# A two-block transformer kernel: three of its linears take both activation parts in one 512-column matmul, and VectorE adds the halves

## The reference

```
x = first_block(x):  proj = rms_norm(x) @ w_in        # 2048 -> 6144; 24 column tiles of 128 here,
                                                      # 24 more as "conv" beside the attention
                     mix  = [attention | gated short conv] @ w_out
                     x += rms_norm(mix);  x += rms_norm((silu(hn @ w_gate) * (hn @ w_up)) @ w_down)
second_block(x):     proj = rms(h) @ w_in_2
                     y_a, y_b = rwkv7(...), fox_attention(...)
                     merged = sigmoid(g_a) * (y_a @ w_branch_a) + sigmoid(g_b) * (y_b @ w_branch_b)
                     h = h + merged @ w_o
                     h = h + (silu(rms(h) @ w_gate) * (rms(h) @ w_up)) @ w_down
```

## Time and profile before

| what | value |
|---|---|
| median of 3 executions | 2859.67 us (2857.73 to 2863.03) |
| profiled execution | 2861.01 us, its span 2859.0 us |
| TensorE busy (matmul) | 2823.2 us, 99% of the span |
| TensorE weight load | 2494.8 us, 87% |
| VectorE busy | 1717.7 us, 60% |
| ScalarE busy | 1226.9 us, 43% |
| DMA | 484.97 MB, mean 170 GB/s |
| granted TensorE clock | 0.998 of full speed over the span |

### The profile page before, as it was taken

The page is one execution under the profiler, slowest core; times in us unless marked ns, Lnnn a source line. Parts: engine busy times, 40 slices in busy tenths (PEclk is TensorE's granted clock), DMA queues, the critical chain, the costliest instruction groups (busy, mean ns, idle before and its releaser), DMA issues.

```text
span 2859.0 us, 49983 instructions
## 1 busy us (share of the span) xinstructions
PE 2823.2 (99%) x20901; PEld 2494.8 (87%) x20901; DVE 1717.7 (60%) x2507; ACT 1226.9 (43%) x1828; POOL 53.1 (2%) x102
## 2 busy tenths in 40 slices
PE   9999999999999999999999999999999999999999
PEld 8999878888888888899788888999998888888887
DVE  6467747666556544654666665766666666565444
ACT  5355544333333444543543443554453333333443
POOL 1000000000000000000000000000000000000000
PEclk9999999999999999999999999999999999999999
DMA  7566455555555555455434335545555555555554
GB/s 246 191 168 180 148 177 162 191 178 189 190 184 183 191 191 190 155 177 163 119 105 125 105 96 162 133 120 192 182 178 188 188 190 177 191 191 163 190 191 147
DMA packets 370319, 484.97 MB, mean 170 GB/s; under 512 B 12360, under 2 KB 181655, under 8 KB 370151
## 3 DMA queue, kind: packets, MB, share of 16 engines
q1 hardware_dynamic: 362752, 471.49, 52.6%
q0 software_dynamic: 4112, 7.88, 1.0%
q10 hardware_dynamic: 3302, 3.39, 0.4%
HBM read 475.70 MB, written 7.01 MB: 169 GB/s over the span
## 4 chain that ended last, share of the span: by engine, by line
PE 89%; DVE 7%; ACT 2%; issue 1%; DMA 1%; DVEq 0%; SPq 0%; ACTq 0%
PE psum L353 20%; PE psum L355 10%; PE psum L565 6%; PE psum L357 5%; PE psum L359 5%; PE psum L358 5%; PE psum L569 5%; PE psum L567 5%; PE psum L694 4%; PE psum L696 4%; PE psum L695 4%; PE psum L763 3%; PE psum L762 3%; PE psum L764 3%; DVE w_lo L343 3%
## 5 line engine op out<-in xcount | busy, mean ns | idle before, releaser
L343 DVE TENSOR_TENSOR w_lo<-w_raw,w_hi 128x1024 fp32r<-128x1024 f32 x728 | 859.6, 1222 | 817.0 <-ACT w_hi L334 817.0
L334 ACT ACTIVATE w_hi<-w_raw 128x1024 fp32r<-128x1024 f32 x728 | 733.0, 1054 | 1160.0 <-PE psum L355 587.1
L353 PE MATMUL psum<-act,w_hi 128*128 128x512 f32 x2816 | 989.8, 394 | 5.1 <-DVE w_lo L343 2.6
L355 PE MATMUL psum<-act,w_lo 128*128 128x256 f32 x2816 | 790.8, 281 | 0.0
L353 PEld LDWEIGHTS psum<-act,w_hi 128*128 128x128 f32 x2816 | 529.6, 188 | 132.4 <-DVE w_lo L343 12.1
L355 PEld LDWEIGHTS psum<-act,w_lo 128*128 128x128 f32 x2816 | 530.1, 188 | 0.1
L357 PE MATMUL psum<-act,w_hi 128*128 128x256 f32 (+3 forms) x1360 | 387.9, 285 | 3.5 <-DVE w_lo L343 3.5
L565 PE MATMUL psum<-act,w_hi 128*128 128x256 f32 (+1 forms) x1280 | 387.5, 303 | 0.3 <-issue 0.3
L359 PE MATMUL psum<-act,w_lo 128*128 128x256 f32 (+3 forms) x1360 | 387.1, 285 | 0.0
L358 PE MATMUL psum<-act,w_hi 128*128 128x256 f32 (+3 forms) x1360 | 387.0, 285 | 0.0
L569 PE MATMUL psum<-act,w_lo 128*128 128x256 f32 (+1 forms) x1280 | 360.9, 282 | 0.0
(11 more groups left out here) (397 smaller groups left out, 2767.7 us busy)
## 6 DMA issues: line engine op xcount, KB each, us to landing
w_raw<-w_in SPq DMA_DIRECT2D x128, 1024.0 KB, 5.8
w_raw<-w_down SPq DMA_DIRECT2D x88, 1024.0 KB, 5.1
w_raw<-w_gate_up SPq DMA_DIRECT2D x88, 1024.0 KB, 5.1
w_raw<-w_gate SPq DMA_DIRECT2D x44, 1024.0 KB, 5.2
w_raw<-w_up SPq DMA_DIRECT2D x44, 1024.0 KB, 5.2
w_raw<-w_out SPq DMA_DIRECT2D x16, 1024.0 KB, 5.3
w_raw<-w_o SPq DMA_DIRECT2D x16, 1024.0 KB, 5.0
w_raw<-w_branch_a SPq DMA_DIRECT2D x8, 1024.0 KB, 5.1
```

Of the source, the lines that this page charges most:

```text
L334: nc.scalar.activation(w_hi[:, s % 2, 2 * h:2 * h + 2, 0:wd], w_raw[:, s % RAW, 2 * h:2 * h + 2, 0:wd], ACT.Copy).then_inc(hi_ready, 1)
L343: nc.vector.tensor_tensor(w_lo[:, s % 2, 2 * h:2 * h + 2, 0:wd], w_raw[:, s % RAW, 2 * h:2 * h + 2, 0:wd], w_hi[:, s % 2, 2 * h:2 * h + 2, ...
L353: pe.matmul(dst.rearrange("p (h n) -> p h n", h=2), w1, both_parts, start=first, stop=False, skip_group_check=True)
L355: return pe.matmul(dst[:, 0:n], w0, act_hi[:, k, tok], start=False, stop=last, skip_group_check=True)
```

## The change

`w_in` (the first 24 tiles of the input linear), `branch` and `w_o` join the list of wide linears. Their tiles take 512 columns of PSUM. The evacuations add the halves:

- `w_in`: four tensor_reduce of 512 to 256 columns and one multiply of the four tiles by rstd, in the place of four multiplies. The mixer waits for the multiply (`proj_done`) and not for `acc_free`.
- `branch`: for each tile a tensor_reduce into SBUF, a wait for it, and a multiply by the gate in SBUF, in the place of one multiply out of PSUM.
- `w_o`: for each tile an add of the lower half to the residual, a wait for it, and an add of the upper half, in the place of one add.

```diff
-        wide = [L[n] for n in ("ffn", "ffn2")]
+        wide = [L[n] for n in ("w_in", "ffn", "branch", "w_o", "ffn2")]
...
-        def take_tiles(lin, i, g, dst, op1=None):
-
-            for m in range(4):
-                wait_tile(lin, i, g, m)
-                nc.vector.tensor_tensor(dst(m), psum[:, first_bank(lin, i, g) + m, 0:SEQ], rstd[:, X],
-                                        ALU.mult).then_inc(acc_free, 1)
-
...
+        proj_done = sem("proj_done")
...
             side(4)
-            pe.wait_ge(acc_free, L["w_in"].t1)
+            pe.wait_ge(proj_done, L["w_in"].iters)
...
-            tiles = [(psum[:, first_bank(lin, 0, 0) + m, 0:SEQ], m * P, P, m) for m in range(4)]
+            tiles = [(psum[:, first_bank(lin, 0, 0) + m], m * P, P, m) for m in range(4)]
...
+        by_gates, half_added, sums_added = sem("by_gates"), sem("half_added"), sem("sums_added")
...
                 b = first_bank(lin, i, g) + m
-                v.tensor_tensor(dst, psum[:, b:b + 1, 0:SEQ], gate_tiles[KT * g + 4 * i + m], ALU.mult) \
-                    .then_inc(acc_free, 1)
+                v.tensor_reduce(dst.rearrange("p k n -> p (k n)"), psum[:, b].rearrange("p (h n) -> p n h", h=2),
+                                AX, ALU.add).then_inc(acc_free, 1)
+                v.wait_ge(acc_free, lin.t0 + 8 * i + 4 * g + m + 1)
+                v.tensor_tensor(dst, dst, gate_tiles[KT * g + 4 * i + m], ALU.mult).then_inc(by_gates, 1)
             if g == 1:
-                v.wait_ge(acc_free, lin.t0 + 8 * i + 8)
+                v.wait_ge(by_gates, 8 * i + 8)
                 part = merged[:, 4 * i:4 * i + 4]
                 v.tensor_tensor(part, part, gated, ALU.add).then_inc(merged_done, 1)
...
                 t, b = res[:, bass.ds(4 * i + m, 1), X], first_bank(lin, i, g) + m
-                v.tensor_tensor(t, psum[:, b:b + 1, 0:SEQ], t, ALU.add).then_inc(acc_free, 1)
+                v.tensor_tensor(t, psum[:, b:b + 1, 0:SEQ], t, ALU.add).then_inc(half_added, 1)
+                v.wait_ge(half_added, 4 * i + m + 1)
+                v.tensor_tensor(t, psum[:, b:b + 1, SEQ:2 * SEQ], t, ALU.add).then_inc(acc_free, 1)
...
-                take_tiles(lin, i, g, lambda m: proj[:, bass.ds(4 * i + m, 1), :])
+                add_halves(lin, i, g, lambda m: proj[:, bass.ds(4 * i + m, 1), :].rearrange("p k n -> p (k n)"))
+                part = proj[:, bass.ds(4 * i, 4), :]
+                v.wait_ge(acc_free, lin.t0 + 4 * i + 4)
+                v.tensor_tensor(part, part, rstd[:, X].unsqueeze(1).broadcast_to([P, 4, SEQ]), ALU.mult) \
+                    .then_inc(proj_done, 1)
```

## The result

The changed kernel takes 2865.15 us (median of 16 executions), the kernel before 2858.72 us (16 executions beside them): a ratio of 1.0023, interval 1.0016 to 1.0030, or 6.4 us more. A second set on another chip gave 1.0019 (1.0010 to 1.0028). So the changed kernel is slower, by about the least that can be told. The profiled execution of the changed kernel has a span of 2864.0 us against 2859.0.

A forecast was written before the change was run, and what follows sets the result against it. TensorE, busy 99%, was taken to bound the kernel by its pace and gaps. Terms -5.1 + 1.6 + 0.8 + 3.2 + 1.7 + 1.9 = +4.1 us gave 2863.8 us against the median of 2859.67, range 2859.0 to 2868.0.

The forecast's parts named there:

- The gain, -5.1: w_in, branch, w_o: 55 units counted, each 0.093 us faster when wide, -5.1 us in all.
- End of w_in, nothing: End of w_in: last reduce and multiply end at 167.5, before TensorE asks at 168.26; no loss, cover 0.7 us.
- Inside branch, +1.6 and +0.8: Branch: w_lo 0.53 us late in three second halves, +1.6; first evacuation starts late, +0.8.
- The gap in front of w_o, +3.2: Passage from branch to w_o: w_lo ends at T + 14.01 (T: the mark, ScalarE's w_hi start), 3.2 us late.
- The clock, +1.7: Behind the 3.2 us gap at w_o: clock falls to 0.50, costing 1.7 us; bounds 0 and 3.4.
- an idle of 1.83 us left the clock at 1.00: At 1388 to 1390 in the earlier profile: evidence that gaps shorter than 1.83 us bring no clock fall.
- The passage to ffn2, +1.9: Passage from w_o to ffn2: longer adds uncovered, two gaps of some 1.3 and 0.8 us, +1.9; no clock fall.
- the clock falls more often or longer: Rival, gaps before w_o and ffn2: more low-clock stretches at 1.7 us each, time 2866.3; chance 0.20.
- The dearer wait for VectorE's own result: Rival, branch pairs: waiting costs 0.16 us, not 0.04; sum +7.0, time 2866.7; chance 0.12.
- Everything added is hidden: Rival, all late places: added VectorE work costs nothing, only the gain of -5.1 stays, 2854.6 us; chance 0.13.

The follow-up runs named there:

- e4: The changed kernel once more, nothing altered, run and profiled a second time; 2864.54 us, ratio 1.0019 to the kernel before.
- e8: The changed kernel with the w_lo of w_o's second unit ahead of branch's last evacuation in VectorE's order; 2865.59 us, ratio 1.0025 to the kernel before.
- e2: The changed kernel with only branch wide, w_in and w_o as before; 2865.51 us, ratio 1.0021 to the kernel before.
- e3: The changed kernel with only w_o wide, w_in and branch as before; 2860.36 us, ratio 1.0001 to the kernel before.
- e6: The changed kernel with the last 4 tiles of branch (fourth iteration, second half) narrow; 2861.25 us, ratio 1.0007 to the kernel before.
- e1: The changed kernel with only w_in wide, branch and w_o as before; 2858.10 us, ratio 1.0001 to the kernel before.

## Why the prediction was right, and where not

The forecast was 2863.8 us, and 2865.15 was measured, inside the range; the sum was +4.1 and the medians say +6.4, the marks +5.2 and, in e4, +4.1. I gave a change of no more than 0.2% the larger chance (0.58), and 0.23% came. The mechanism is the one that was forecast, at each of its places: the pace, the late w_lo behind longer evacuations, and a fall of the clock behind the largest gap and not behind the others. That the sum is so near owes something to luck: w_in brought 0.6 us less than counted and branch lost 0.5 us less, which cancel, and the price of the clock was read wrongly. Step by step:

- **The gain, -5.1.** The pace is as forecast: 5.59 us a wide unit, and 1.3 us over the 14 units of w_o. In w_in it was over-counted. From the fifth unit on, 20 units gave 1.4 us and not 1.9; four of them, which share TensorE with other matmuls, went from 7.31 to 7.27 us, 0.05 each; and a first evacuation that I had not worked out by itself holds a unit up a little. VectorE and TensorE there, in the changed kernel:

```profile
52.44 1.22 DVE L3024 TENSOR_TENSOR arena<-arena,rstd 128x1024 f32<-128x1024 f32 x1
53.58 2.35 DVE L343 TENSOR_TENSOR w_lo<-w_raw,w_hi 128x1024 fp32r<-128x1024 f32 x2
55.73 0.28 PE L355 MATMUL psum<-act,w_lo 128*128 128x256 f32 x1
55.99 0.50 PE L353 MATMUL psum<-act,w_hi 128*128 128x512 f32 x1
```

  w_lo ends at 55.93 and TensorE restarts at 55.99, 0.26 after its last start and not 0.12; at the slower restart that follows, some 0.2 us go. The three units before brought 0.07 together: they don't run at the steady pace either (their marks stand 3.8 to 7.7 us apart in the kernel before). It is -1.5 in all for w_in, where I had 23 units and -2.1. What the step left out is those three units, the four shared ones, and the norm's work that stands ahead of this evacuation (a reciprocal of 1.75 us among it).
- **End of w_in, nothing.** Right. The multiply ends at 165.53, and the transposes start at 166.21, one matmul's distance behind the last side quarter; the earlier trace rows had the same order before.

```profile
164.30 1.23 DVE L3024 TENSOR_TENSOR arena<-arena,rstd 128x1024 f32<-128x1024 f32 x1
166.09 0.28 PE L569 MATMUL psum<-act,w_lo 128*128 128x256 f32 x1
166.21 0.49 PE L1314 MATMUL psum<-tab,arena 128*128 128x128 f32 x3
```

- **Inside branch, +1.6 and +0.8.** The first evacuation cost 0.88 (0.8 forecast). The second halves cost 0.49 and 0.47, near the forecast for each (0.53), but two of them and not three: the first finds TensorE held up already. I had added up latenesses that follow one another as if none covered the next.
- **The gap in front of w_o, +3.2.** w_lo ended at T + 13.91 and not T + 14.01, as the pairs took 1.06 us and not 1.08. The idle of 2.98 us in the trace counts from the modelled end of a matmul; from start to start the gap is 3.26, so TensorE was 3.1 late. The third unit was in time, as worked out.
- **The clock, +1.7.** The place was right. The size was 1.5 us in e4 and e8 and 2.6 to 2.7 in the first profile and e2; my upper bound of 3.4 covers it, and in the first profile this is the largest error of the sum. Two readings behind the term were wrong. First, the 1.7 us was work lost at the low clock, not time lost. Where a profile lacks one of these stretches, its marks show what the stretch costs elsewhere: 1.0 us at 421 (e3 and e6), 0.9 at 1177 (e6) and nothing at 453 (the changed kernel, in which TensorE, ahead at first, then waits 0.59 us for VectorE at 456.5). Second, "an idle of 1.83 us left the clock at 1.00" is only the part of an idle that lies in that window. The whole of it, in the kernel before, is 2.17 us, the same as the idle in front of 452.03 that brought a fall:

```profile
1390.35 0.72 PE L1839 MATMUL psum<-arena,tab 128*128 128x272 f32 x2 [2.17 <-DVE arena L2284]
```

  So the rows held no length below which the clock stays and above which it falls.
- **The passage to ffn2, +1.9.** 1.93 to 1.94 in each kernel in which all of w_o is wide. The clock stayed up behind an idle of 1.12 us in all six profiles that have it, as I took it to, though the 1.83 us on which I rested this was misread.

The rivals: "the clock falls more often or longer" came half true, at the first of its two places, and its time of 2866.3 is as near to the result as the forecast. The dearer wait for VectorE's own result did not come: 0.04 us between line 2848's end and line 2851, as in the earlier trace rows. w_o's 1.3 us in 14 units is 5.8 ns a group, as forecast. The Trainium skill (TensorE: Matmul & The Clock Gate, section "Wait — 56ns, not 53.3ns?") gives a fixed cost of about 2.5 ns for a warm matmul. The trace has more: one matmul fewer, together with its weight load, brought 5.8 ns, and no run parts the two. "Everything added is hidden" was wrong by four places. What I had named as showing me wrong, a mark at 5.68, a low clock at ffn2, a passage with no gap, did not appear; a lateness in w_in's marks did, of 0.2 us.

## What to carry to other kernels

When one engine gets shorter work at the price of longer work on another, look at each place where the second engine's longer work stands ahead of something the first waits for, and add up the second's whole queue up to that due time; e8 shows that reordering it doesn't help when the sum doesn't fit. Here all that the wide units won by the marks, some 4.4 us, was no more than what one evacuation at one stage boundary cost (4.5 to 5.8 us). A change like this one is better made group by group, by the cover that each group has, and not by linear.

## What was not expected of the hardware

- **A gap costs more than its length.** 24 matmuls without use in an idle of 3 us made the kernel 2.3 us faster in the medians and the passage 1.5 us shorter by the marks, by holding the clock up.
- **The same idle doesn't always bring the fall.** The four idles of 2.0 to 2.3 us near 420, 450, 1175 and 1205 stand in each of the eleven profiles; behind 40 of these 44 the clock fell to 0.50, and behind four it didn't (near 420 in e3 and e6, near 1175 in e6, near 450 in the changed kernel). The idle of 2.2 us near 1388 stands in all eleven too, and no fall followed in any. An idle of 1.35 us in front of 1572.49 brought one in e6, and 1.26 us one in e1, while 1.23 to 1.81 us at the same place left the clock at 1.00 in four others. First the changed kernel near 450; then e6, near 420 and in front of 1572.49:

```profile
450.11 0.50 PE L353 MATMUL psum<-act,w_hi 128*128 128x512 f32 x1 [2.19 <-DVE w_lo L343]
448.00:456.00 8.00, 5.89 (x31) 4.97 (x32) 7.86 (x12) 2.50 (x3) 0.00 (x0) 1.00 0.39 131
```

```profile
416.00:428.00 12.00, 9.65 (x55) 7.79 (x54) 9.91 (x22) 9.15 (x19) 0.00 (x0) 1.00 0.25 87
1572.49 0.25 PE L1895 MATMUL psum<-arena 32*32 32x32 f32 x4 [1.35 <-issue]
1572.00:1576.00 4.00, 3.51 (x92) 1.89 (x91) 0.93 (x2) 1.13 (x3) 0.00 (x0) 0.59 0.02 4
```

  In e3 the clock fell at 300.5 and again at 307.4, with TensorE busy throughout:

```profile
300.00:304.00 4.00, 4.00 (x21) 3.82 (x20) 2.28 (x6) 0.63 (x1) 0.00 (x0) 0.57 0.20 79
```

  By the marks a stretch of low clock of 3.4 us cost between nothing and 1.5 us (the two of e3 3.1 together), in parts of the program that the change leaves alone. It is not the whole spread: between 1347 and 1915 the six profiles that have no low clock there still differ by 1.9 us. This is the reason why a change of 0.1% is read here from marks and not from times. Why the clock falls in one execution and not in the next was not found.
